# Moving the subtraction of the weights' low parts from GpSimd to VectorE in the retention heads

## The reference, cut to what matters

```python
h = rmsnorm(x, norm_mix[l]).astype(f32) * (1.0 + sc1) + sh1
q, k, v, g, u, vv = jnp.split(h @ ab_w_in[e].astype(f32), ab_cuts, axis=-1)
...
mod = (jax.nn.silu(cond.astype(f32)) @ mod_w[l].astype(f32) + mod_b[l].astype(f32))[:, None, :]
```

## Time and profile before

| | |
|---|---|
| time, median of 3 runs | 2556.89 us (2554.69 to 2560.3) |
| the profiled execution's own time | 2559.11 us |
| its span, first to last instruction | 2557.3 us |
| PE busy | 2492.9 us, 97% of the span |
| DVE busy | 1884.7 us, 74% |
| POOL busy | 902.3 us, 35% |
| granted PE clock over the span | 0.989 |
| w_lo made by POOL, blocks of 128 x 1024 | 42 at L746 in the whole program, 2.35 to 3.55 us each |

### The profile page before, as it was taken

How to read it: one execution, slowest core, us unless ns; L and a number is a source line. 1 busy time by engine, 2 the same in 40 slices (tenths; PEclk the granted TensorE clock), 3 DMA queues, 4 the chain that set the end, 5 groups by cost and what they waited for, 6 DMA issues and landing times.

```text
span 2557.3 us, 43627 instructions
## 1 busy us (share of the span) xinstructions
PE 2492.9 (97%) x15458; PEld 2436.8 (95%) x15458; DVE 1884.7 (74%) x2893; ACT 922.4 (36%) x1494; POOL 902.3 (35%) x757
## 2 busy tenths in 40 slices
PE   7999999998999999999999999999999999999998
PEld 6999999998999999999999888799999999999997
DVE  6878878779888788888868898947756656656674
ACT  5333322223332332332324666713432432332323
POOL 1221212322545544544531000122545545535530
PEclk9999999999999999999999999999999999999999
DMA  7422322342223122222133111132111111111131
GB/s 259 153 72 71 89 66 81 132 146 79 65 70 94 58 78 86 66 78 78 58 124 111 41 41 41 56 122 83 41 42 49 41 41 49 41 41 54 36 124 75
DMA packets 238666, 200.18 MB, mean 78 GB/s; under 512 B 9461, under 2 KB 229365, under 8 KB 236918
## 3 DMA queue, kind: packets, MB, share of 16 engines
q1 hardware_dynamic: 236580, 179.43, 22.5%
q10 hardware_dynamic: 2002, 19.65, 2.0%
HBM read 174.92 MB, written 24.13 MB: 78 GB/s over the span
## 4 chain that ended last, share of the span: by engine, by line
PE 85%; DVE 10%; issue 2%; ACT 1%; DMA 0%; POOL 0%; SPq 0%; DVEq 0%; ACTq 0%; POOLq 0%
PE psum L879 55%; PE psum L1187 24%; PE psum L1237 2%; DVE mod_sum L1781 2%; DVE h_lo L1831 1%; PE psum L1143 1%; DVE sumsq L1840 1%; DVE b_sum L1918 0%; DVE pair_sum L1811 0%; DVE s_bwd L2174 0%; DVE sumsq L1752 0%; DVE x L1855 0%; DVE xc L2284 0%; DVE mod_sum L1776 0%; DVE v_raw L2217 0%
## 5 line engine op out<-in xcount | busy, mean ns | idle before, releaser
L879 PE MATMUL psum<-h_hi,w_hi 128*128 128x384 f32 (+1 forms) x2880 | 673.0, 342 | 17.9 <-POOL w_lo L746 5.7
L879 PE MATMUL psum<-h_lo,w_hi 128*128 128x384 f32 (+1 forms) x2880 | 659.8, 337 | 0.0
L879 PE MATMUL psum<-h_hi,w_lo 128*128 128x384 f32 (+1 forms) x2880 | 659.6, 337 | 0.0
L879 PEld LDWEIGHTS psum<-h_hi,w_hi 128*128 128x128 f32 x2880 | 514.3, 189 | 32.8 <-issue 19.4
L1956 DVE TENSOR_TENSOR x<-x,psum 128x576 f32<-128x576 f32 x560 | 407.0, 751 | 175.4 <-PE psum L1187 172.8
L879 PEld LDWEIGHTS psum<-h_lo,w_hi 128*128 128x128 f32 x2880 | 518.7, 189 | 0.0
L879 PEld LDWEIGHTS psum<-h_hi,w_lo 128*128 128x128 f32 x2880 | 518.1, 189 | 0.0
L1187 PE MATMUL psum<-b_hi,w_hi 128*128 128x288 f32 x1568 | 336.9, 297 | 2.0 <-DVE even_raw L1906 2.0
L1187 PE MATMUL psum<-b_hi,w_lo 128*128 128x288 f32 x1568 | 336.5, 296 | 0.0
L1187 PE MATMUL psum<-b_lo,w_hi 128*128 128x288 f32 x1568 | 336.3, 296 | 0.0
L809 POOL TENSOR_TENSOR w_lo<-w_sum,w_hi 128x256 fp32r<-128x256 f32 x168 | 155.6, 929 | 324.6 <-ACT w_hi L1463 323.9
(11 more groups left out here) (309 smaller groups left out, 2975.9 us busy)
## 6 DMA issues: line engine op xcount, KB each, us to landing
w_raw<-in_mlp_w SPq DMA_DIRECT2D x128, 512.0 KB, 3.9
pair_raw<-in_mod_w SPq DMA_DIRECT2D x96, 256.0 KB, 2.8
mod_raw<-in_mod_w SPq DMA_DIRECT2D x64, 256.0 KB, 2.9
w_raw<-in_ab_w_in SPq DMA_DIRECT2D x24, 512.0 KB, 4.6
x_spill<-x ACTq DMA_DIRECT2D x2, 4608.0 KB, 14.0
x_old<-x_spill SPq DMA_DIRECT2D x16, 576.0 KB, 5.6
w_raw<-in_lru_w_in SPq DMA_DIRECT2D x16, 512.0 KB, 4.2
x_spill<-x ACTq DMA_DIRECT2D x4, 1728.0 KB, 6.8
```

The source lines that it names most:

```text
L879: mm = pe.matmul(psum[:, s, c, 0:end - c * CH], w, v[:, k, c * CH:end], start=(first and n == 0 and w is hi[k] and v is in_hi), stop=(last ...
```

## The change

In the heads POOL no longer makes `w_lo`. It makes the first two units' parts as before, then only casts (`high`), and after its 22 casts waits until all 24 of the heads' low parts are made. DVE makes the other 22 low parts at six points of its order in a head: `next_weights(n)` makes that of the unit two ahead of unit n. The last head leaves out the last two points, since the output projection's first units stay with POOL.

```diff
             with pool.Fori(1, outs) as i:
-                split(i, 0)
-                split(i, 1)
+                high(i, 0)
+                high(i, 1)
+            pool.wait_ge(split_done, AT_OUT[0].units + 2)
             split(outs, 0)
...
+            def high(i, s):
+
+                pool.wait_ge(raw_landed[s], at(i, 16, 16))
+                pool.wait_ge(unit_done, i * 2 + (s - 1))
+                pool.sem_inc(passed, 1)
+                pool.tensor_copy(w_hi[:, s, :], w_raw[:, s, :]).then_inc(hi_done, 1)
...
+            def weights_low(i, per, c):
+
+                s = c % 2
+                dve.wait_ge(hi_done, at(i, per, c + 1))
+                dve.wait_ge(split_done, at(i, per, c + 2))
+                dve.tensor_tensor(w_lo[:, s, :], w_raw[:, s, :], w_hi[:, s, :].bitcast(F32), ALU.subtract).then_inc(split_done, 1)
...
+                def next_weights(n):
+                    weights_low(h, HEAD_UNITS, U0 + n + 2)
...
                 scale_out(s, 0, turned, float(P) ** -0.5).then_inc(read_out[s], 1)
                 next_mod(0)
+                next_weights(0)
...
                 dve.tensor_scalar(by_bank(k_bwd[:]), whole(s), col(k_dec[:, 1, :], h), None, ALU.mult).then_inc(read_out[s], 1)
+                next_weights(1)
                 next_mod(1)
                 next_mod(2)
                 unit(2)
                 dve.wait_ge(k_ready, h + 1)
                 s = (I0 + 3) % 2
                 scale_out(s, 2, turned).then_inc(read_out[s], 1)
+                next_weights(2)
                 next_mod(3)
...
                 last.then_inc(read_out[s], 1)
+                next_weights(3)
                 next_mod(4)
                 unit(4)
                 s = (I0 + 9) % 2
                 scale_out(s, 4, kT).then_inc(read_out[s], 1)
+                if not last_head:
+                    next_weights(4)
                 next_mod(5)
...
                 scale_out(s, 5, k_fwd).then_inc(read_out[s], 1)
+                if not last_head:
+                    next_weights(5)
                 next_mod(7)
```

More of the change, by code:

```diff
@@ L834, in _ @@
             blocks = AT_MIX[1].units // 2
[L836 to L841, removed]
             with pool.Fori(AT_MIX[1].units // 2, blocks + 1) as i:
@@ L2303, in output_gate @@
                 scale_out(s, 1, gate_raw).then_inc(read_out[s], 1)
[L2305 to L2310, removed]
             def mix_low(start, end):
@@ L2337, in lru_block @@
                     if more == 2:
-                        weights_low(b, 4)
+                        weights_low(b, BLK_UNITS, U0 + 4)
                 else:
@@ L2366, in lru_block @@
                     input_out(b + 2, b, BLK_NEXT_X, 3)
-                    weights_low(b, 5)
+                    weights_low(b, BLK_UNITS, U0 + 5)
                 dve.tensor_tensor(work_b[1][:], work_b[1][:], work_b[0][:], ALU.add).then_inc(dve_step, 1)
@@ L2377, in _ @@
             input_out(0, None, 0, 0)
-            weights_low(None, 2)
+            weights_low(None, 0, U0 + 2)
             steps.enter(None, 6)
@@ L2382, in _ @@
             input_out(1, None, 1, 1)
-            weights_low(None, 3)
+            weights_low(None, 0, U0 + 3)
             dve.wait_ge(x_spilled, 16 * (2 + SPILLS[0]))
```

## The result

The changed kernel takes 2567.02 us (median of 6 runs, 2563.35 to 2569.43), the kernel before 2559.24 us on the same chip (6 runs, 2554.69 to 2560.82). The ratio is 1.0035, 95% interval 1.0025 to 1.0046, so about 9 us slower (the two medians differ by 7.8 us). I had forecast 2562.0, at most 2566.5, starting from 2556.89 for the kernel before: a rise of 5.1 us, at most 9.6. The direction of the sum was right, its size was not, and the time is just outside the range. Of the 5.0 us by which the time misses the forecast, 2.4 are that the kernel before itself came out higher than the 2556.89 that I started from; the rest is the rise.

The account below looks back on a forecast made before the run. PE, busy 97% of the span, was taken as the bound. Terms 1.6 + 2.5 + 1.3 gave +5.4 us, or +4.1 if the clock holds: 2562.3 or 2561.0 on the median, written as 2562.0, range 2557.0 to 2566.5.

Parts of the forecast that it names:

- Point 1: DVE's subtraction ahead of mods 1 and 2 delays unit 2's read-out: +0.9, +0.8, +0.3 us in heads 1-3, -0.4 in head 0.
- point 4: Subtraction ahead of mod 5 waits for POOL's cast of the next head's unit 0; +2.5 us, about 1.4 if landings take 4.0.
- point 5: Subtraction ahead of mod 7 waits some 5 us for the cast of the next head's unit 1; hidden by unit 0's product.
- Head 1's term of +1.5: PE's start behind mod 5 in head 1 moves from 241.27 to 242.7, with the load taking 5.0 us to land.
- The clock: Longer PE waits for mod 5 may bring 3.41 us stretches at lower clock, 1.5 us each; 0.9 of one counted, +1.3 us.
- my fourth rival: The clock falls at two or three head boundaries: +4.1 and 3 to 4.5 us, 2564 to 2566; chance 0.17.
- the third: Rival: the wait ahead of mod 7 isn't covered and delays the next head; +3 to +6 us, 2565 to 2568; chance 0.08.
- Points 0, 2, 3 and 5: Subtractions behind units 0, 2 and 3, and ahead of mod 7: hidden from PE, no cost in the sum.
- The first rival: Quiet beside DVE wins if the next head's unit 0 lands in about 2 us: -2.3 us, 2554.6; chance 0.08.

Follow-up runs that it names:

- e6: The changed kernel, but in head 0 alone POOL makes unit 3's low part again, heads 1 to 3 as changed; ratio 1.0025 to the kernel before.
- e8: The changed kernel with DVE making low parts only behind units 0 and 2, POOL the others as in the kernel before; ratio 1.0042.

## Why the prediction was right in direction and wrong in size

**Point 1 is the step that failed**: "In head 0 ... 2.1 us of quiet less 1.13 lets DVE catch up ... about -0.4 (0 to -0.7). Sum of point 1: +1.6 us." Measured by ratio it is +5.9 (alone) to +6.4 us (undone). What it had wrong is head 0: I let the quiet beside mod 1 win there and put DVE's wait for the cast at nothing, and DVE stood idle for it for 3.8 us. In PE's waits head 0 went from 0.22 + 0.73 to 3.10 + 0.73, +2.9 instead of -0.4; heads 1, 2 and 3 gained 0.72, 0.64 and 0.31, where I had 0.9, 0.8 and 0.3. So three heads were right within 0.2 us, and head 0 alone was wrong. Of its +2.9, 1.0 to 1.4 us are left when it is set against e6 and e8, where PE came as early; the rest is that it came late in the profiled execution of before. With heads 1 to 3 that makes some 3 of the 5.9 to 6.4 us. Lower clock is the likeliest rest (with point 1 alone PE had 7 us of it in head 0, before none), but that is argued. I had asked for the cast's time at point 4 and point 5, but not at point 1, where in heads 1 to 3 it is early. In head 0 of the profiled execution of before it came at 83.61 and ended at 84.65, while DVE was done with `k_bwd` at 84.6: no margin at all. In the changed kernel DVE was there 2 us sooner, while the load landed 1.7 us later (issued 1.7 us sooner, it took 3.4 us longer), behind the store of x. The quiet that I credited came only after the waiting.

**Point 4**: the mechanism was right and its waits smaller than forecast. DVE's idle time was 1.5, 2.0 and 2.0 us (forecast 1 to 3), mod 5 took 4.3 us, and PE's waits grew by 0.2, 0.3 and 0.4 us in heads 0 to 2, some 1.1 us with the last head's 0.2, against 2.5. Head 1's term of +1.5 was mis-sized, as its load took 3.8 us to land and not the 5.0 of the earlier trace rows. "If all three landings take 4.0 us it is about 1.4" was nearer. The saving when points 4 and 5 are undone, 3.6 us, is more than those waits.

**The clock**: I counted 0.9 of one stretch, +1.3 us; three came, at 1.4 to 1.5 us each, 4.4 us. In the profiled execution the heads' 10.8 us are thus 4.6 + 1.1 of waits, 4.4 of clock and 0.7 of small differences. That is read from one execution of each kernel; that the clock costs the same in the others is not shown, and that point 4's 3.6 us are 1.1 of waits and one or two stretches is argued. By mechanism my fourth rival (2564 to 2566, which I gave 0.17) is nearest to the outcome: two of three boundaries had a lower stretch. The number itself lies in the range of the third (2565 to 2568), but only by chance, since PE didn't wait for what point 5 delays.

**Points 0, 2, 3 and 5** cost nothing, as written: point 5's idle time was 5.15, 3.95 and 4.09 us and PE didn't notice, and 5.9 for point 1 and 3.6 for points 4 and 5 already make 9.5 us, all of the 9.0 within the uncertainty. Point 3 moved or not makes no difference (0.9982 and 0.9979). For points 0 and 2 alone there is no clean run.

**The first rival**, that the quiet wins, was refuted as the change stands: its condition, a landing in about 2 us, didn't come (3.7 to 3.8 us). But its mechanism is real: with points 1, 4 and 5 placed later the same work on DVE is 0.2% faster than before (0.9979).

## What to carry to other kernels

When an instruction is put into a hand-written order, look up when its input is ready in every copy of the loop, the first above all: here the start-up's store made the first pass different, and the input was late unseen, since nobody but a side engine waited for it. Look also at how much such a margin moves from execution to execution: the cast was 0 us late in the one that I had read, and 4 us in six others. Put the instruction behind the next piece of work that doesn't need it, so that this work covers the input's lateness: the same 22 subtractions gave 1.0035 ahead of the sums and 0.998 behind them. Moving the large transfer out of one load's way put it into another's.

## What the runs showed of the hardware that was not expected

- A wait's length did not decide whether the lower clock followed. In head 2 a wait of 1.73 us was followed by it in the changed kernel, and one of 1.70 us in the run with point 1 later was not (1.00 in both windows behind it):

```profile
344.00:347.40 3.40, 3.40 (x25) 1.00 0.29 78
347.40:350.80 3.40, 3.40 (x21) 1.00 0.00 0
```

  Waits of 1.46 and 1.58 us were followed by it in other runs, 1.50 and 1.66 were not.
- The one load of 512 KB took 4.7 to 5.5 us to land with the 4.7 MB store issued behind it (three runs) and 8.3 to 12.2 us with it issued ahead (eleven runs). In these eleven it landed 2.9 to 3.5 us behind the store.
- e8_only_0_2 lost most of 11.7 us in a stage 200 us behind the edit, in unchanged code, with POOL's work lying otherwise beside DVE's there; what set that off stays open.
